# Queries and first gate features of a sparse-attention layer as rounded halves, gate columns first

## The chip, the cores and the metric

The kernel runs on one core of one Trainium2 chip. The metric is the device time of one execution in microseconds (us), lower is better. A run of a kernel gives one such time; the time given for a kernel is the median of its runs.

## The reference, cut to what matters

The reference is one inference step of a small decoder with one mLSTM layer and one sparse-attention layer (NSA), for a prompt of 512 rows and a sample group of 8 x 4 = 32 rows that share every weight. Everything is float32. The change lies in the first part of the attention layer, for all 544 rows x (1024 features each):

```python
h = rmsnorm(x)                        # here: rows x, as 8 slices of 128 features x 544 rows
up = h @ w_in                         # w_in: 1024 x (1024 queries | 3 x 1024 gate features | 48 branch gates)
q  = up[:, 0:1024]                    # 16 heads of 64
z  = silu(up[:, 1024:4096])           # one set of 1024 per branch: compressed, selected, window
g  = sigmoid(up[:, 4096:4144])        # one weight per branch and head
s  = q . kcmp * scale                 # 31 compressed keys per row
p  = masked_softmax(s)
o_cmp = p @ vcmp                      # compressed branch
y  = sum over branches of g * z * o   # later: the selected and window branches, then y @ w_out
```

## The kernel before, in words

The program is a row of stages. Each stage is one block with a program for each of the engines, and a block's end is a barrier for the engines that it uses. Engines meet through semaphores. Big weights come as 28 chunks of up to 2 MB (`weight_chunks`, L63), loaded by SyncE (SP) into a ring of two slots in turn (`wring`, slot = chunk number modulo 2); `load_chunks` (L88) waits, before it loads chunk c, for the last use of chunk c-2 (`chunk_last`), and an engine that reads a chunk waits in `chunk` (L107). PSUM banks go round: `open_bank` (L115) takes the next of `nring` banks (6 in this part) and waits until its former user has emptied it.

Matrix products are done in two ways. Where both operands are float32, one call of the program becomes two weight loads and two passes, so that the trace has two records for each call. In several other stages the operands are split ahead: ScalarE (ACT) rounds a float32 tile to float32r ("high"), VectorE (DVE) subtracts and keeps the rest ("low"), and three float32r products (high x high, high x low, low x high) are added in PSUM, each with one record. The stage of the mLSTM gate path, `stage_gate` (L1200), does it so: its products are L1238 to L1240, its roundings L1259 (weights, 1024 columns) and L1263 (rows, 544 columns), its rests L1280 and L1284.

The stages that the change touches:

- `stage_compress` (L1817) makes the compressed keys and values. At its end SP has already issued the loads of chunks 17 and 18, whose slots are free early.
- `stage_query` (L2053): 8 query pieces of 128 features (chunks 17 and 18, four each), each as two groups of rows (256 and 288), each group 8 float32 calls (L2066); then the 48 branch-gate columns (chunk 19) for five row tiles by `project_rows` (L2072, products at L1317). ACT empties each query bank (L2115, L2120, scaled) and applies the sigmoid to the gates (L2126). DVE only clears `QS`; POOL builds masks. SP loads chunks 19, 20 and 21, each once its slot is free.
- `stage_cmp_branch` (L2238): scores against compressed keys (L2263, L2270), gate features of branch 0, first half (`z_features`, L2142, four pieces, chunk 20), transposes of the weights P (L2278), second half of the gate features (chunk 21), the samples' sums (L2287), and then for each of 8 head pairs t a product that spreads the softmax sums' reciprocals over features (L2297, bank `cR`) and the product P x V (L2303, bank `cP`). DVE makes masked scores, maxima and differences (L2337 to L2348), then sums and reciprocals (L2353 to L2357), copies the transposed P (L2362), and for each t multiplies `cR` by z (L2371) and the result by `cP` (L2374). ACT does the exponentials (L2320) and silu (L2175, L2177). SP loads chunks 22 and 23, then stores the samples' rows in 8 transfers (L2313).
- `stage_keys` (L2377) does the selected and window branches in 64 steps, and the gate features of branches 1 and 2 (chunks 22 to 25) by `z_features` at its start and `z_blocks` between steps. In a gate-feature bank of the kernel before, one call makes 64 features, two of them side by side in the array.

The order of work on an engine is the order of the program text. A chunk's load is one DMA of 128 x 8 rows of 2 KB, by the call

```python
sp.dma_start(dst, src).then_inc(k.chunk_here[c % NW], 16)
```

## Time and profile before

| what | value |
|---|---|
| median of 3 runs | 1504.17 us (1503.64 to 1505.37) |
| the profiled execution's own time | 1504.39 us |
| its span in the trace | 1502.6 us |
| TensorE busy | 1396.2 us, 93% |
| VectorE, ScalarE, GpSimd busy | 50%, 34%, 13% |
| mean granted TensorE clock | 0.96 |
| stage_query | about 943 to 1015 us of the span |
| stage_cmp_branch | about 1015 to 1109 us |

Times are microseconds from the span's start unless marked ns. PE is TensorE's matmul, PEld its weight loads, which overlap PE. "PEq", "SPq" are the engines' sequencers. The mean of one matmul record holds its whole pipeline; records overlap, so what a matmul costs is read from the starts of successive ones or from a group's busy time over its calls. "Idle before, releaser" is the time an engine waited and what ended it; "<-PEq L2871" is the release at a block's end.

### The profile page before, as it was taken

The page shows a single profiled execution, that of the slowest core. Times are in us where ns is not written, and L with a number is a line of the kernel's source. Part 1 is how long each engine was busy: PE and PEld are TensorE (multiplying, and loading weights), DVE is VectorE, ACT ScalarE, POOL GpSimd, SP SyncE. Part 2 cuts the span into 40 slices and gives each one's busy share as a digit, 9 for nine tenths or more (in the row PEclk, how much of TensorE's full clock was granted, in tenths as well). Part 3 has the DMA queues.
Part 4 walks back from the last instruction along what each step waited for, and adds up shares of the span by engine and source line. Part 5 has one row for each costly group of instructions (what it writes and reads, how often), then busy time and mean ns, then how long its engine had stood idle before and what let it go on. Part 6 is the DMA issues. An engine that isn't in the chain of part 4 may idle for free. (4 is left out here: it accounts for less than half of the span.)

```text
span 1502.6 us, 24705 instructions
## 1 busy us (share of the span) xinstructions
PE 1396.2 (93%) x9357; PEld 1002.6 (67%) x9357; DVE 743.9 (50%) x1575; ACT 515.8 (34%) x1227; POOL 189.6 (13%) x231
## 2 busy tenths in 40 slices
PE   4899899999996699999799999999999999999978
PEld 4899655454542599777577999787666555555456
DVE  4676446676755732625633231005034656565646
ACT  5232524242421332423522231122104545454542
POOL 5221041313130100000110110100000000010020
PEclk9999999999998799999899999997999999999999
DMA  6431236767677522222443340011141314141221
GB/s 188 167 113 56 72 105 225 252 221 256 222 257 261 212 84 86 85 102 87 146 170 120 102 165 11 3 60 58 57 124 33 122 52 141 60 113 63 43 93 60
DMA packets 93835, 182.06 MB, mean 121 GB/s; under 512 B 10855, under 2 KB 24835, under 8 KB 92515
## 3 DMA queue, kind: packets, MB, share of 16 engines
q1 hardware_dynamic: 90998, 164.88, 33.4%
q0 software_dynamic: 2720, 15.60, 3.1%
q8 instruction: 76, 1.25, 0.3%
q14 instruction: 41, 0.34, 0.1%
HBM read 133.82 MB, written 54.95 MB: 126 GB/s over the span
## 5 line engine op out<-in xcount | busy, mean ns | idle before, releaser
L1022 DVE SCALAR_TENSOR_TENSOR wring<-wring,nbw,ps 128x512 f32<-128x512 f32 x128 | 86.9, 742 | 59.8 <-PE ps L673 59.7
L2160 PE MATMUL ps<-xnT,wring 128*64 128x256 f32 (+1 forms) x768 | 101.3, 400 | 1.9 <-DVEq L2662 1.7
L2615 ACT ACTIVATE P<-ps,nmx 128x128 f32<-128x128 f32 (+3 forms) x128 | 66.3, 522 | 95.4 <-DVE nmx L2648 95.4
L2142 PE MATMUL ps<-xnT,wring 128*64 128x256 f32 (+1 forms) x768 | 90.4, 398 | 1.3 <-PEq L2874 1.3
L1417 PE MATMUL ps<-wh,xl 128*128 128x512 f32 x224 | 88.1, 393 | 0.0
L416 PE MATMUL ps<-xuh,wuh 128*128 128x256 f32 (+1 forms) x256 | 77.6, 303 | 11.3 <-DVE wring_low L363 10.3
L1238 PE MATMUL ps<-xh,wh 128*128 128x256 f32 (+1 forms) x256 | 75.0, 293 | 7.2 <-DVE xl L1284 7.1
L2142 PEld LDWEIGHTS ps<-xnT,wring 128*64 128x64 f32 x768 | 59.0, 139 | 32.2 <-issue 3.8
L2648 DVE TENSOR_REDUCE nmx<-ps 128x1 f32<-128x128 f32 (+3 forms) x128 | 56.8, 486 | 47.0 <-PE ps L2479 40.8
L417 PE MATMUL ps<-xul,wuh 128*128 128x256 f32 (+1 forms) x256 | 76.3, 298 | 0.0
L418 PE MATMUL ps<-xuh,wring_low 128*128 128x256 f32 (+1 forms) x256 | 76.3, 298 | 0.0
L1239 PE MATMUL ps<-xl,wh 128*128 128x256 f32 (+1 forms) x256 | 74.3, 290 | 0.0
L1240 PE MATMUL ps<-xh,wl 128*128 128x256 f32 (+1 forms) x256 | 73.9, 289 | 0.0
L2160 PEld LDWEIGHTS ps<-xnT,wring 128*64 128x64 f32 x768 | 50.9, 136 | 31.9 <-issue 8.4
L1902 PE MATMUL ps<-cRh,cwh 128*128 128x384 f32 x192 | 67.5, 352 | 0.0
L1370 DVE TENSOR_TENSOR wring_low<-wring,wh 128x512 fp32r<-128x512 f32 x64 | 41.1, 687 | 53.2 <-PE ps L1381 53.2
L1903 PE MATMUL ps<-cRl,cwh 128*128 128x384 f32 x192 | 65.4, 341 | 0.0
L1904 PE MATMUL ps<-cRh,cwl 128*128 128x384 f32 x192 | 65.4, 340 | 0.0
L2066 PE MATMUL ps<-xnT,wring 128*128 128x256 f32 (+1 forms) x256 | 60.6, 401 | 2.2 <-PEq L3096 2.2
L416 PEld LDWEIGHTS ps<-xuh,wuh 128*128 128x128 f32 x256 | 51.3, 200 | 11.8 <-issue 5.3
L2762 POOL TENSOR_TENSOR arena<-arena,tmp 128x512 f32<-128x512 f32 x16 | 20.3, 1271 | 303.5 <-DVEq L2689 303.5
L2066 PEld LDWEIGHTS ps<-xnT,wring 128*128 128x128 f32 x256 | 49.7, 195 | 12.8 <-issue 2.3
(489 smaller groups left out, 3135.3 us busy)
## 6 DMA issues: line engine op xcount, KB each, us to landing
wring<-in_state_C_dram SPq DMA_DIRECT2D x64, 512.0 KB, 5.2
out_dram<-wring SPq DMA_DIRECT2D x64, 512.0 KB, 5.3
wring<-in_a_w_up_dram SPq DMA_DIRECT2D x8, 2048.0 KB, 8.6
wring<-in_b_w_in_dram SPq DMA_DIRECT2D x8, 2048.0 KB, 9.1
wring<-in_a_w_down_dram SPq DMA_DIRECT2D x4, 2048.0 KB, 8.6
craw<-in_cache_kv_dram SPq DMA_DIRECT2D x64, 128.0 KB
arena<-in_cache_kv_dram SPq DMA_DIRECT2D x32, 256.0 KB, 3.9
arena<-in_cache_win_dram SPq DMA_DIRECT2D x8, 1024.0 KB, 6.0
```

What stands on the lines that cost most here:

```text
L416: pe.matmul(b[:, 0:t1 - t0], w_hi, x_hi, start=kt == 0, stop=False)
L417: pe.matmul(b[:, 0:t1 - t0], w_hi, x_lo, start=False, stop=False)
L418: m = pe.matmul(b[:, 0:t1 - t0], w_lo, x_hi, start=False, stop=kt == KD - 1)
L1022: dve.scalar_tensor_tensor(out=c, in0=c, scalar=nbws[:, h % 2, 2 * S + s:2 * S + s + 1], in1=b[:, :], op0=ALU.mult, op1=ALU.add).then_inc( ...
L1238: pe.matmul(out, w_hi, x_hi, start=kt == 0, stop=False)
L1239: pe.matmul(out, w_hi, x_lo, start=False, stop=False)
L1240: m = pe.matmul(out, w_lo, x_hi, start=False, stop=kt == KD - 1)
L1417: m = pe.matmul(b, x_lo, w_hi, start=False, stop=last and kt == KD - 1)
L1902: pe.matmul(b[:, 0:CROW], w_hi, r_hi, start=j == 0, stop=False)
L2066: m = pe.matmul(b[:, 0:t1 - t0], w[:, kt, 128 * m4:128 * m4 + 128], k.xnT[:, kt, t0:t1], start=kt == 0, stop=kt == KD - 1)
L2142: m = pe.matmul(b[64 * par:64 * par + 64, 0:t1 - t0], w[:, kt, x:x + DH], k.xnT[:, kt, t0:t1], start=kt == 0, stop=kt == KD - 1)
L2160: m = pe.matmul(k.ps[64 * par:64 * par + 64, bank, 0:t1 - t0], w[:, kt, x:x + DH], k.xnT[:, kt, t0:t1], start=kt == 0, stop=kt == KD - 1)
```

## The change

1. The order of chunks 17 to 19: the 48 gate columns come first (17), then the two query chunks (18, 19).
2. The 8 query pieces and the 8 gate-feature pieces of branch 0 are done as high and low halves, three float32r products of 128 features (`InHalves`, pieces p = 0 to 15). ACT rounds the rows (8 x 544 columns) and each weight piece (1024 columns), DVE makes the rests; high weights have two slots, low weights are written over the chunk itself. In `stage_query` pieces 0 and 1 are prepared at the start, piece m+2 after the bank of piece m is emptied; in `stage_cmp_branch` ACT rounds piece t+10 after the silu of piece t, and DVE takes its part between softmax steps.
3. The branch gates are projected ahead of the queries.
4. Chunks 20 to 25 (`GATES`: the gate features of all three branches) come as 16 transfers each: [128 partitions, 4 runs, 64 values], so that the two 64-feature halves of a pair lie next to each other.
5. In the compressed branch DVE multiplies P by reciprocal x gate before the transposes (`cr_ready`); the products and banks `cR` and the multiplication by z of those are gone.

The diff, cut to its core:

```diff
--- before.py
+++ after.py
@@ -70,7 +70,7 @@
             out.append(cols(k.w_down[1024 * half:1024 * half + 1024, :], 512 * n, 512))
     out += [cols(k.w_kv, 512 * c, 512) for c in range(3)]
     out += [k.cmp_w1[s].rearrange("(j p) n -> p j n", p=128) for s in range(2)]
-    out += [cols(k.w_in, 0, 512), cols(k.w_in, 512, 512), cols(k.w_in, 4096, 48)]
+    out += [cols(k.w_in, 4096, 48), cols(k.w_in, 0, 512), cols(k.w_in, 512, 512)]
...
 CH_UP, CH_DOWN, CH_KV, CH_CMP, CH_IN, CH_OUT, CH_END = 0, 8, 12, 15, 17, 26, 28
+GATES = range(CH_IN + 3, CH_OUT)
 def load_chunks(sp, k, lo, hi):
@@ -95,6 +96,13 @@
             bank, n_full = k.chunk_last[c - NW]
             sp.wait_ge(k.half_done if bank == "half" else k.w_low if bank == "low" else k.bank_full[bank], n_full)
+        if c in GATES:
+            for par in range(2):
+                for kt in range(KD):
+                    sp.dma_start(dst[:, kt].rearrange("p (hh a d) -> p a hh d", a=2, d=DH)[:, par],
+                                 src[:, kt, 256 * par:256 * par + 256].rearrange("p (hh d) -> p hh d", d=DH)).then_inc(k.chunk_here[c % NW], 16)
+            continue
...
@@ -107,7 +115,8 @@
 def chunk(pe, k, c):
     src = k.chunks[c]
-    pe.wait_ge(k.chunk_here[c % NW], 16 * (c // NW + 1) + (48 if c >= CH_OUT else 0))
+    loads = sum(2 * KD if e in GATES else 4 if e >= CH_OUT else 1 for e in range(c % NW, c + 1, NW))
+    pe.wait_ge(k.chunk_here[c % NW], 16 * loads)
...
@@ -2050,24 +2059,77 @@
+class InHalves:
+    def __init__(self, k, xh, xl, wh):
+        self.k, self.xh, self.xl, self.wh = k, xh, xl, wh
+    def cols(self, p, w):
+        return w[:, :, 128 * (p % 4):128 * (p % 4) + 128]
+    def chunk_no(self, p):
+        return CH_IN + 1 + p // 4
+    def high(self, p):
+        return self.wh[:, p % 2]
+    def low(self, p):
+        return self.cols(p, self.k.wring_low[:, self.chunk_no(p) % NW, :].rearrange("p (a b) -> p a b", b=512))
+    def key(self, p, hf):
+        return ("q", p, hf) if p < 8 else ("z", 0, p - 8, hf)
+    def round_x(self, act, kt):
+        act.activation(self.xh[:, kt, :], self.k.xnT[:, kt, :], ACT.Copy).then_inc(self.k.xq_high, 1)
+    def rest_x(self, dve, kt):
+        dve.wait_ge(self.k.xq_high, kt + 1)
+        dve.tensor_tensor(self.xl[:, kt, :], self.k.xnT[:, kt, :], self.xh[:, kt, :], ALU.subtract).then_inc(self.k.xq_low, 1)
+    def round_w(self, act, p):
+        w = self.cols(p, chunk(act, self.k, self.chunk_no(p)))
+        if p >= 2:
+            bank, n = self.k.bank_of[self.key(p - 2, 1)]
+            act.wait_ge(self.k.bank_full[bank], n)
+        act.activation(self.high(p), w, ACT.Copy).then_inc(self.k.wq_high, 1)
+    def rest_w(self, dve, p):
+        w = self.cols(p, chunk(dve, self.k, self.chunk_no(p)))
+        dve.wait_ge(self.k.wq_high, p + 1)
+        dve.tensor_tensor(self.low(p), w, self.high(p), ALU.subtract).then_inc(self.k.wq_low, 1)
+    def piece(self, pe, p):
+        k = self.k
+        pe.wait_ge(k.wq_low, p + 1)
+        low = self.low(p)
+        for hf, (t0, t1) in enumerate(HALF):
+            b, full = open_bank(pe, k, self.key(p, hf))
+            for kt in range(KD):
+                if p == 0 and hf == 0:
+                    pe.wait_ge(k.xq_low, kt + 1)
+                x_hi, x_lo = self.xh[:, kt, t0:t1], self.xl[:, kt, t0:t1]
+                out = b[:, 0:t1 - t0]
+                pe.matmul(out, self.wh[:, p % 2, kt, :], x_hi, start=kt == 0, stop=False)
+                pe.matmul(out, self.wh[:, p % 2, kt, :], x_lo, start=False, stop=False)
+                m = pe.matmul(out, low[:, kt], x_hi, start=False, stop=kt == KD - 1)
+            m.then_inc(full, 1)
+        k.chunk_last[self.chunk_no(p)] = k.bank_of[self.key(p, 1)]
 def stage_query(nc, k, ctx):
     block = ctx.enter_context(nc.Block())
     SCALE = float(DH) ** -0.5
+    hq = k.hq
     @block.tensor
     def _(pe):
-        for c in range(2):
-            w = chunk(pe, k, CH_IN + c)
-            for m4 in range(4):
-                for hf, (t0, t1) in enumerate(HALF):
-                    b, full = open_bank(pe, k, ("q", 4 * c + m4, hf))
-                    for kt in range(KD):
-                        m = pe.matmul(b[:, 0:t1 - t0], w[:, kt, 128 * m4:128 * m4 + 128], k.xnT[:, kt, t0:t1],
-                                      start=kt == 0, stop=kt == KD - 1)
-                    m.then_inc(full, 1)
-            k.chunk_last[CH_IN + c] = k.bank_of[("q", 4 * c + 3, 1)]
-        project_rows(pe, k, "bg", k.xnT, CH_IN + 2, 1)
+        project_rows(pe, k, "bg", k.xnT, CH_IN, 1)
+        for p in range(8):
+            hq.piece(pe, p)
...
+        hq.round_x(act, 0)
+        hq.round_w(act, 0)
+        for kt in range(1, KD):
+            hq.round_x(act, kt)
+        hq.round_w(act, 1)
+        for i in TILES:
+            r = 128 if i < NT else S
+            b, free = full_bank(act, k, ("bg", i))
+            act.activation(k.gt[0:r, i, :], b[0:r, 0:3 * H], ACT.Sigmoid).then_inc(free, 1)
         act.wait_ge(k.q_clear, 1)
         for m in range(8):
             g = m // 2
@@ -2120,14 +2191,18 @@
                             x = act.activation(k.QS[d0:d0 + 64, odd:SB:2, g, 16 * odd + hh:16 * odd + 16:HPG], rows[:, odd:SB:2, :],
                                                ACT.Copy, scale=SCALE)
                 x.then_inc(free, 1)
-        for i in range(NT + 1):
-            r = 128 if i < NT else S
-            b, free = full_bank(act, k, ("bg", i))
-            act.activation(k.gt[0:r, i, :], b[0:r, 0:3 * H], ACT.Sigmoid).then_inc(free, 1)
+            hq.round_w(act, m + 2)
     @block.vector
     def _(dve):
+        hq.rest_x(dve, 0)
+        hq.rest_w(dve, 0)
+        for kt in range(1, KD):
+            hq.rest_x(dve, kt)
+        hq.rest_w(dve, 1)
         dve.memset(k.QS[:, :, :, :], 0.0).then_inc(k.q_clear, 1)
+        for m in range(8):
+            hq.rest_w(dve, m + 2)
 def z_bank(pe, k, br, c, n):
@@ -2138,7 +2213,7 @@
     b, full = open_bank(pe, k, ("z", br, HPG * c + hh, hf))
     for kt in range(KD):
         for par in range(2):
-            x = 256 * par + DH * hh
+            x = 128 * hh + DH * par
             m = pe.matmul(b[64 * par:64 * par + 64, 0:t1 - t0], w[:, kt, x:x + DH], k.xnT[:, kt, t0:t1],
                           start=kt == 0, stop=kt == KD - 1)
     m.then_inc(full, 1)
...
@@ -2243,9 +2313,9 @@
     Sc = sb("Sc", [128, NT + 1, H, 32])
     Pc = sb("Pc", [128, NT + 1, H, 32])
     PcT = k.kvT.rearrange("p a t -> p (a t)")[:, 0:(NT + 1) * 4 * 128].rearrange("p (i g t) -> p i g t", i=NT + 1, g=4)
-    mx = sb("cmx", [128, NT + 1, H])
-    sm = sb("csm", [128, NT + 1, H])
-    zr = sb("czr", [128, 2, T])
+    x0 = (NT + 1) * D + (NT + 1) * 4 * 128
+    mx, sm = (k.arena[:, x0 + n * (NT + 1) * H:x0 + (n + 1) * (NT + 1) * H].rearrange("p (i h) -> p i h", h=H) for n in range(2))
+    hq = k.hq
     block = ctx.enter_context(nc.Block())
     def heads_of(t):
@@ -2270,14 +2340,16 @@
                 m = pe.matmul(b[32 * g:32 * g + 32, 32 * s:32 * s + NCMP], k.QS[:, s, g, :], k.kcT[:, s, g // 2, :],
                               start=True, stop=True)
         m.then_inc(full, 1)
-        z_features(pe, k, 0, 0)
+        for p in range(8, 12):
+            hq.piece(pe, p)
         for i in range(NT + 1):
-            pe.wait_ge(k.cp_ready, i + 1)
+            pe.wait_ge(k.cp_ready if i == NT else k.cr_ready, i + 1)
             b, full = open_bank(pe, k, ("cT", i))
             for g in range(G if i < NT else 2):
                 m = pe.transpose(b[:, 128 * g:128 * g + 128], Pc[:, i, 4 * g:4 * g + 4, :].rearrange("p h n -> p (h n)"), k.ident[:, :])
             m.then_inc(full, 1)
-        z_features(pe, k, 0, 1)
+        for p in range(12, 16):
+            hq.piece(pe, p)
         drained(pe, k, ("cT", NT))
         for r in range(4):
@@ -2287,16 +2359,9 @@
                     m = pe.matmul(b[32 * g:32 * g + 32, DH * a:DH * a + DH], PcT[32 * r:32 * r + NCMP, NT, a, 32 * g:32 * g + 32],
                                   k.vcS[32 * r:32 * r + NCMP, a, DH * g:DH * g + DH], start=True, stop=True)
             m.then_inc(full, 1)
-        pe.wait_ge(k.cr_ready, 1)
         for i in range(NT):
             drained(pe, k, ("cT", i))
         for t in range(KD):
-            b, full = open_bank(pe, k, ("cR", t))
-            for i in range(NT):
-                for par, h in enumerate(heads_of(t)):
-                    m = pe.matmul(b[64 * par:64 * par + 64, 128 * i:128 * i + 128], sm[:, i, h:h + 1].to_broadcast([128, DH]),
-                                  k.ident[:, :], start=True, stop=True)
-            m.then_inc(full, 1)
             b, full = open_bank(pe, k, ("cP", t))
             for par, h in enumerate(heads_of(t)):
                 g, hh = h // HPG, h % HPG
@@ -2318,8 +2383,11 @@
             act.wait_ge(k.cs_ready, i + 1)
             n = H if i < NT else SB
             act.activation(Pc[:, i, 0:n, :], Sc[:, i, 0:n, :], ACT.Exp).then_inc(k.cp_ready, 1)
-        z_silu(act, k, 0, 0)
-        z_silu(act, k, 0, 1)
+        for t in range(KD):
+            for hf in range(2):
+                z_silu_bank(act, k, 0, t // HPG, t % HPG + HPG * hf)
+            if t < 6:
+                hq.round_w(act, t + 10)
     @block.vector
     def _(dve):
@@ -2355,11 +2423,17 @@
             st.then(dve.reciprocal(m_, m_))
             if i < NT:
                 st.then(dve.tensor_tensor(m_, m_, k.gt[:, i, 0:H], ALU.mult))
-        dve.sem_inc(k.cr_ready, 1)
+                dve.tensor_tensor(Pc[:, i, :, :], Pc[:, i, :, :], m_.unsqueeze(2).to_broadcast([128, H, 32]),
+                                  ALU.mult).then_inc(k.cr_ready, 1)
+            if i in (1, 3):
+                hq.rest_w(dve, 10 + i // 2)
+        hq.rest_w(dve, 12)
         for i in range(NT + 1):
             n = G if i < NT else 2
             b, free = full_bank(dve, k, ("cT", i))
             dve.tensor_copy(PcT[:, i, 0:n, :], b[:, 0:128 * n].rearrange("p (g t) -> p g t", g=n)).then_inc(free, 1)
+        for p in range(13, 16):
+            hq.rest_w(dve, p)
         for r in range(4):
             b, free = full_bank(dve, k, ("cO", r))
             dve.tensor_tensor(k.osb[:, r:SB:4, :], b[:, 0:2 * DH].rearrange("p (a d) -> p a d", d=DH),
@@ -2367,11 +2441,8 @@
         for t in range(KD):
             for hf in range(2):
                 drained(dve, k, ("z", 0, t, hf))
-            b, free = full_bank(dve, k, ("cR", t))
-            st.then(dve.tensor_tensor(zr[:, t % 2, :], b[:, :], k.z[:, t, :], ALU.mult))
-            dve.sem_inc(free, 1)
             b, free = full_bank(dve, k, ("cP", t))
-            dve.tensor_tensor(k.y[:, t, 0:T], b[:, :], zr[:, t % 2, :], ALU.mult).then_inc(free, 1)
+            dve.tensor_tensor(k.y[:, t, 0:T], b[:, :], k.z[:, t, :], ALU.mult).then_inc(free, 1)
 def stage_keys(nc, k, ctx):
@@ -2868,11 +2939,16 @@
         k.identb = sb("identb", [128, 128], BF16, where=att)
         k.causb = sb("causb", [128, 128], BF16, where=att)
         k.newb = sb("newb", [128, NQ * S + 4], BF16, where=att)
-        with ExitStack() as c:
-            k.mtmp = sb("mtmp", [128, 132 + NQ * S], where=c)
-            stage_query(nc, k, c)
-        with ExitStack() as c:
-            stage_cmp_branch(nc, k, c)
+        with ExitStack() as rows:
+            k.hq = InHalves(k, rows.enter_context(nc.sbuf_tensor("xh5", [128, KD, TA], F32R)),
+                            over(nc, "xl5", [128, KD, TA], k.at["arena"]),
+                            rows.enter_context(nc.sbuf_tensor("wh5", [128, 2, KD, 128], F32R)))
+            with ExitStack() as c:
+                k.mtmp = sb("mtmp", [128, 132 + NQ * S], where=c)
+                stage_query(nc, k, c)
+            with ExitStack() as c:
+                stage_cmp_branch(nc, k, c)
         with ExitStack() as c:
             stage_keys(nc, k, c)
     with ExitStack() as c:
```

## Rows read from the trace of the kernel before

**Rows 1.** The page: busy time, share of the span and instructions of each engine

```profile
PE 1396.2 (93%) x9357; PEld 1002.6 (67%) x9357; DVE 743.9 (50%) x1575; ACT 515.8 (34%) x1227; POOL 189.6 (13%) x231
```

**Rows 2.** PE in order of time: start, length, line, operands, count of records

```profile
1004.37 10.25 PE L1317 MATMUL ps<-wring,xnT 128*32 128x48 f32 x80
1015.61 13.86 PE L2263 MATMUL ps<-cmp_rows,Qp 64*128 64x31 f32 x128 [0.99 <-PEq L2871]
...
1030.42 3.89 PE L2142 MATMUL ps<-xnT,wring 128*64 128x256 f32 x18
...
1109.52 29.55 PE L2142 MATMUL ps<-xnT,wring 128*64 128x256 f32 x256 [1.28 <-PEq L2874]
```

**Rows 3.** PE groups by line, window 943 to 1016, then 1015 to 1110

```profile
L2066 PE MATMUL ps<-xnT,wring 128*128 128x256 f32 (+1 forms) x256 | 60.6, 401 | 2.2 <-PEq L3096 2.2
...
L2297 PE MATMUL ps<-ident,csm 128*64 128x128 f32 x128 | 8.6, 273 | 0.0
L2303 PE MATMUL ps<-arena,cmp_rows 128*64 128x512 f32 x32 | 8.5, 592 | 0.0
```

**Rows 4.** PE in order of time in stage_gate: float32r products, first of each group

```profile
550.24 0.30 PE L1238 MATMUL ps<-xh,wh 128*128 128x288 f32 x1
...
553.44 0.28 PE L1238 MATMUL ps<-xh,wh 128*128 128x256 f32 x1
...
556.27 0.30 PE L1238 MATMUL ps<-xh,wh 128*128 128x288 f32 x1
```

**Rows 5.** ACT in order of time: roundings, then the end of a query piece

```profile
505.99 4.47 ACT L1263 ACTIVATE xh<-xnT 128x544 fp32r<-128x544 f32 x8
...
520.59 1.05 ACT L1259 ACTIVATE wh<-wring 128x1024 fp32r<-128x1024 f32 x1
...
1004.47 0.38 ACT L2115 ACTIVATE Qp<-ps 64x256 f32<-64x256 f32 x1 [3.12 <-PE ps L2066]
...
1005.30 0.25 ACT L2120 ACTIVATE QS<-ps 64x16 f32<-64x16 f32 x2
```

**Rows 6.** DVE in order of time: rests in stage_gate, the last score difference

```profile
507.26 6.73 DVE L1284 TENSOR_TENSOR xl<-xnT,xh 128x544 fp32r<-128x544 f32 x5
...
527.70 1.23 DVE L1280 TENSOR_TENSOR wl<-wring,wh 128x1024 fp32r<-128x1024 f32 x1 [0.52 <-ACT wh L1259]
...
1033.74 0.43 DVE L2348 TENSOR_TENSOR Sc<-Sc,cmx 128x256 f32<-128x256 f32 x1
```

**Rows 7.** Windows: us, PE, PEld, DVE, ACT, POOL busy, PEclk, DMA share, GB/s

```profile
944.50:946.00 1.50, 1.50 (x7) 1.28 (x6) 0.35 (x1) 0.00 (x0) 1.07 (x4) 0.74 0.00 0
...
1006.50:1008.00 1.50, 1.50 (x16) 1.50 (x15) 0.00 (x0) 0.56 (x2) 0.00 (x0) 1.00 1.01 345
...
1012.50:1014.00 1.50, 1.50 (x9) 1.50 (x9) 0.00 (x0) 0.00 (x0) 0.00 (x0) 0.50 0.00 0
...
1033.50:1035.00 1.50, 1.50 (x14) 0.94 (x12) 1.37 (x4) 0.78 (x2) 0.00 (x0) 0.85 0.00 0
```

**Rows 8.** SP in order of time, then one source's durations (min/median/max ns)

```profile
1014.65 0.37 SPq L104 DMA_DIRECT2D wring<-in_b_w_in_dram  x1
...
1094.70 4.26 SPq L2313 DMA_DIRECT2D sample_rows<-osb  x8
...
1317.06 3.13 SPq L101 DMA_DIRECT2D wring<-in_b_w_out_dram  x4
...
L101 SPq DMA_DIRECT2D wring<-in_b_w_out_dram x4: 618/665/1056, 1317.1 to 1319.6; - x4
```

**Rows 9.** The mLSTM stage's end: POOL in order of time, ACT's wait (us, times, longest)

```profile
497.93 0.54 POOL L903 DMA_DIRECT2D out_dram<-nprow  x1
...
ACT wh L1259 <- PEq L3069: 4.9, 1, 4.9
```

**Rows 10.** DMA issues: KB each, median us from issue to landing

```profile
wring<-in_b_w_in_dram SPq DMA_DIRECT2D x1, 192.0 KB, 2.8
...
out_dram<-nprow POOLq DMA_DIRECT2D x1, 8.0 KB, 5.1
```

More of the change, by code:

```diff
@@ L2158, in z_blocks @@
         for par in range(2):
-            x = 256 * par + DH * hh
+            x = 128 * hh + DH * par
             m = pe.matmul(k.ps[64 * par:64 * par + 64, bank, 0:t1 - t0], w[:, kt, x:x + DH], k.xnT[:, kt, t0:t1],
@@ L2178, in z_silu_bank @@
     m.then_inc(free, 1)
-def z_silu(act, k, br, c):
-    for n in range(2 * HPG):
-        z_silu_bank(act, k, br, c, n)
 def z_ready(eng, k, br, c):
@@ L3012, in build @@
         k.xr_low = sem("xr_low")
+        k.xq_high = sem("xq_high")
+        k.xq_low = sem("xq_low")
+        k.wq_high = sem("wq_high")
+        k.wq_low = sem("wq_low")
         k.w_high = sem("w_high")
```

## The prediction

> **What bounds the kernel now.** The page first: TensorE (PE) is busy for 93% of the span, no other engine for more than half [rows 1], so time is won where PE's calls get shorter or fewer and lost where PE stands still. Then the two stages that the change touches, by line and in order of time. `stage_query` is 60.6 us of query products [rows 3] and 10.25 us of gate columns [rows 2]; `stage_cmp_branch` is 14.8 us of scores (1015.61 to 1030.42, [rows 2]), eight pieces of gate features, 2 us of transposes and a tail. Between the stages' borders PE has next to no gap, so its order and its durations give the time, as long as nobody feeds it late. Last the windows of 1.5 us: in and behind the gate columns the granted clock is 0.50, half of 2.4 GHz [rows 7], so each moved part has to be priced at the clock that it will find.
>
> **1. The products as halves.** Four float32 pieces at full clock take 29.55 us [rows 2], 7.39 each (the query pieces 60.6 / 8 = 7.58, with a cold start in it [rows 3]). The float32r price is in `stage_gate`, which makes the same shapes: 24 products of 288 columns, from 550.24 to 553.44, take 3.20 us, 24 of 256 from there to 556.27 take 2.83 [rows 4]. A piece becomes 6.03 us with all three products: 1.36 less for each of 16, **21.7 us**.
>
> Can the others keep up? ACT empties a piece's second group in 1.1 us (from 1004.47, [rows 5]) and rounds the next weights in 1.05 [rows 5], DVE takes 1.23 for the rest [rows 6]: 3.4 us from the end of piece m to piece m+2's weights, and PE works 6.03 us on m+1. Hidden, with 2.6 to spare. At the stage's start ACT needs 4.5 + 2 x 1.05 = 6.6 us. DVE took 6.73 / 5 = 1.35 a slice for rests while POOL worked beside it [rows 6]; all eight at that and two weights are 13.3 us, the upper end; without POOL a slice should be 544/1024 of 1.23, 0.65, the lower end 7.7. POOL's masks fill only the first 6 us: I take 10 to 11. The cover is the gate columns, now first; without it 10 us would show. In the branch, piece 10 waits for ACT behind the last exponential and for DVE behind two softmax tiles, some 7 us after the last score difference at 1034.2 [rows 6], at 1041; PE reaches it at about 1044. Piece 11 is due at 1047 and wanted at 1050. The four multiplications of P lie in the same cover. Nothing, and 3 us of slack.
>
> **2. Gate columns first.** Before, they ran at full clock with 16 records per 1.5 us, at half with 9 and then 8.7 on average [rows 7]. Behind the sparse end of `stage_compress` the clock fell at about 945 already [rows 7] and came back only since dense products followed. Now none follow until the 80 records are through: 16 at full clock, 64 at half, 1.5 + 11.0 = 12.5 us for 10.25, **+2.2**. Then piece 0 runs about 3.5 us cold, as the gate features did from 1030.4 to 1034 [rows 2, 7]: +1.75, against 1.5 that the queries lost before, **+0.2**. Pieces 0 to 7 end at 943.85 + 12.5 + 48.2 + 1.75 = 1006.3; before, PE's work in the stage ended at 1014.6 [rows 2].
>
> **3. The 16 transfers of a chunk.** This term decides. Chunks 20 to 25 come as 16 DMAs each instead of one. Landing is no trouble: 1024 pieces of 192 bytes landed in 2.8 us, fixed part included [rows 10], so 8192 of 256 bytes take at most 8 times that, 22 us, and likelier 10 to 15; each of these chunks is wanted 18 us or more after its issue, chunk 20 by PE only 30 us after. The Trainium skill ("DMA: Bandwidth & Descriptors", the table at its head) has a rule against this change, that runs below 512 bytes are read, modified and written; the sum would not move by it, while no run here shows such runs at line rate.
>
> What is not hidden is SP's own time. A chunk's single issue takes 0.37 us [rows 8]. The 4 of a w_out chunk, with a split destination, took 3.13, 0.78 each, the 8 stores of 256-byte rows 4.26, 0.53 each [rows 8]. The new form has 128 partitions of short runs like the stores and a split destination like w_out, whose median is 0.665: I take **0.55 us each, 8.8 us a chunk**; ends 0.37 and 0.78. By the Trainium skill (the same page, the DGE table's 512 cycles per DMA of earlier generations, at 1.2 GHz) it would be an estimated 0.43 us and 6.8 us a chunk, and the result 4 us lower.
>
> Who stands behind it? Chunk 21 may only start when piece 7 is done, chunk 23 when piece 15 is, both at the end of a stage. Before, that place cost one issue: 1014.65 + 0.37 = 1015.02, and PE started at 1015.61 [rows 2, 8]. A block's end waits for every engine: at the mLSTM stage's end ACT stood 4.9 us for POOL's last store [rows 9], issued at 497.93 and landed 5.1 us later [rows 10].
> - First border: SP is through at 1006.3 + 8.8 = 1015.1, ACT and DVE at +3.4. PE starts 0.6 later, 1015.7, where it started before. All of the 8.3 us won in `stage_query` is waited away, and 9 us of standstill lets the clock fall, so the scores take 14.8 as before.
> - Second border: SP's 8.8 and the stores' 4.3 us [rows 8] follow each other, 13.1 plus 0.6. Before, the stores ended at 1098.96, 10 us ahead of the next stage. PE's own tail is 1 us of sample sums and at most 8.5 of cP, the **8.6 of cR** being gone [rows 3]; it and the 16 DVE products of the tail, now 8, would end at 9 to 10 us.
>
> **4. The branch in sequence.** From 1015.7: scores 14.8, pieces 8 to 11 24.1 + 1.75 cold, transposes 2.1, pieces 12 to 15 24.1: 1082.6. Border 13.7: 1096.3, where the next stage started at 1109.5 [rows 2]: 13.2 earlier. PE stands 4 to 5 us before it, the clock falls, and some 4 us of products run at half: 2 us given back. Elsewhere (chunks 22, 24, 25) the 16 issues lie in waits of over 20 us between SP's loads: nothing, and up to 5 us if a load of sample rows came late by them.
>
> **The sum.** 21.7 - 2.2 - 0.2 + 8.6 is 28 us of PE work; at the borders some 15 of it are waited away and 2 go into the clock: **11 us** are left. The profiled execution took 1504.4, so 1493.2; the median lies 0.2 lower: **1493**. A difference of 0.2%, 3 us, is about what a measurement of this kernel tells from none.
>
> **Rivals.**
> - *The borders don't bind (0.2).* For it: 0.37 us is the commonest issue and no row has the new form; against: both rows with split or short runs are over 0.5. At 0.37 each border is 2.9 us shorter: 1487. If SP does not hold the block at all: first border 3.4 + 0.6, 5.3 us won; pieces 8 to 15, 10.7; tail 10 for the 16.3 between 1093.2 and 1109.5, 6.3: together 22, **1482**. With some full clock left for the scores, 1478.
> - *SP's queue is full (0.1, the other side).* The engines' work on 512 pieces holds up each issue. The place is the same two borders, 32 issues; with 11 us to lose it decides from 0.55 + 11/32 = 0.90 us per issue. For it: one w_out issue took 1.06 us [rows 8]. At that price each border is 8.1 us longer: 1493 + 16 = **1509**. Against: 1024 pieces in 2.8 us are 1.4 for 512 with the fixed part, well under 1 without.
> - *Halves starve (0.08).* DVE or ACT come late for pieces 0, 10 or 11, by 2 to 4 us each beyond the slack above. It gives 1497 to 1501.
>
> The rest, 0.62, is the forecast; its own range is 0.45 to 0.75 us per issue, 1490 to 1500. For 8 in 10 the cheap border is added below and the starved halves above: **1482 to 1501**. Faster by over 3 us: 0.62, 0.2 less a little, and half of the third, less some of its upper edge: 0.82; same 0.08; slower 0.10.
>
> **What would show it.** Right: float32r products 118 and 133 ns apart; gate columns 12 to 13 us with the clock at 0.50; ACT and DVE done 3 to 4 us after piece 7, PE idle some 9 us, and SP's 16 issues ending 0.6 us ahead of the scores; at the second border 16 issues and then the 8 stores as the last thing. Wrong: 16 issues in under 6 or over 12 us; a stage starting before SP is through; PE waiting for low weights between pieces; a high clock in the scores.

## The result, and the profile after

| what | before | after |
|---|---|---|
| median of 4 runs | 1504.47 us (1503.64 to 1505.37) | 1495.27 us (1494.29 to 1495.76) |
| ratio, with its 95% interval | | 0.9936 [0.9923, 0.9949] |
| the profiled execution's own time | 1504.39 us | 1495.41 us |
| its span | 1502.6 us | 1493.7 us |
| mean granted TensorE clock | 0.96 | 0.953 |

The changed kernel is 9.2 us faster; the forecast was 1493.0, with 1482 to 1501 around it. The page, first part, to be held against [rows 1]:

```profile
PE 1374.5 (92%) x9229; PEld 1011.5 (68%) x9229; DVE 765.4 (51%) x1595; ACT 535.2 (36%) x1251; POOL 193.0 (13%) x231
```

PE is busy for 21.7 us less, and only 8.9 of them show in the span; the mean clock has fallen too. (That this is the 21.7 of the prediction's step 1 is chance: the removed `cR` products are in it, and products that a lower clock made longer.) Where the rest went is seen in PE's rows in order of time (start, length, line, operands, records, idle before them and its releaser), the same places as [rows 2]:

```profile
945.26 14.31 PE L1326 MATMUL ps<-wring,xnT 128*32 128x48 f32 x80 [2.42 <-PEq L3176]
...
1018.52 3.84 PE L2333 MATMUL ps<-cmp_rows,Qp 64*128 64x31 f32 x34 [9.24 <-PEq L2947]
...
1084.12 0.97 PE L2359 MATMUL ps<-cmp_rows,arena 31*32 31x64 f32 x64
1085.03 7.09 PE L2368 MATMUL ps<-arena,cmp_rows 128*64 128x512 f32 x32
1098.29 1.98 PE L2217 MATMUL ps<-xnT,wring 128*64 128x256 f32 x8 [6.17 <-PEq L2950]
```

Two standstills, 9.24 us ahead of the scores and 6.17 ahead of `stage_keys`, stand where the kernel before had 0.99 and 1.28. Both end with "PEq", the release at a block's end. Who was last in the block is seen in the durations of the new line's issues (min/median/max in ns, first to last), window 1008 to 1020 and window 1083 to 1099, and in SP in order of time behind the second:

```profile
L103 SPq DMA_DIRECT2D wring<-in_b_w_in_dram x16: 367/507/508, 1009.3 to 1017.4; - x16
...
L103 SPq DMA_DIRECT2D wring<-in_b_w_in_dram x16: 368/507/1249, 1084.2 to 1093.3; - x16
...
DMA to landing us min/median/max: 2.3/3.0/3.3
```

```profile
1094.00 3.69 SPq L2378 DMA_DIRECT2D sample_rows<-osb  x8
1098.82 2.67 SPq L2267 DMA_DIRECT2D osall<-sample_rows  x8
```

An issue takes SP 0.507 us (the median; the first took 0.37). The sixteenth of chunk 21 ends at 1017.9, and the scores start 0.6 later. At the second border the 16 issues are followed by the 8 stores to 1097.69, and the next stage starts 0.6 after those. The granted clock around both (windows: us, PE, PEld, DVE, ACT, POOL busy, PEclk, DMA share, GB/s):

```profile
1013.50:1015.00 1.50, 0.00 (x0) 0.00 (x0) 0.00 (x0) 0.00 (x0) 0.00 (x0) 0.50 1.09 239
...
1094.00:1095.50 1.50, 0.00 (x0) 0.00 (x0) 0.00 (x0) 0.00 (x0) 0.00 (x0) 1.00 1.21 234
1098.50:1100.00 1.50, 1.50 (x8) 0.88 (x8) 0.07 (x1) 0.00 (x0) 0.00 (x0) 0.50 0.03 10
```

In the first of these windows nothing works but SP and the transfers, and the clock has fallen to 1.2 GHz; in the second it is still high. Behind the second standstill the products of `stage_keys` also start at 1.2 GHz.

### The profile page after: what moved, and what is told of

The parts are those of the page before. It is cut to its first block and busy times, and to the rows that moved or that the text cites. A ratio compares the mean times of both kernels' runs of the same rounds, so it can differ in the third digit from the quotient of the medians.

```text
span 1493.7 us, 24597 instructions
## 1 busy us (share of the span) xinstructions
PE 1374.5 (92%) x9229; PEld 1011.5 (68%) x9229; DVE 765.4 (51%) x1595; ACT 535.2 (36%) x1251; POOL 193.0 (13%) x231
## 5 line engine op out<-in xcount | busy, mean ns | idle before, releaser
L2235 PE MATMUL ps<-xnT,wring 128*64 128x256 f32 (+1 forms) x768 | 101.3, 400 | 1.5 <-DVEq L2733 1.3
L425 PE MATMUL ps<-xuh,wuh 128*128 128x256 f32 (+1 forms) x256 | 78.9, 308 | 11.3 <-DVE wring_low L372 10.7
L1247 PE MATMUL ps<-xh,wh 128*128 128x256 f32 (+1 forms) x256 | 75.0, 293 | 7.1 <-DVE xl L1293 7.0
L2115 PE MATMUL ps<-xh,wh 128*128 128x256 f32 (+1 forms) x256 | 74.9, 293 | 0.0
L2116 PE MATMUL ps<-xl,wh 128*128 128x256 f32 (+1 forms) x256 | 74.9, 293 | 0.0
L2117 PE MATMUL ps<-xh,wring_low 128*128 128x256 f32 (+1 forms) x256 | 74.6, 291 | 0.0
L1248 PE MATMUL ps<-xl,wh 128*128 128x256 f32 (+1 forms) x256 | 74.3, 290 | 0.0
L2235 PEld LDWEIGHTS ps<-xnT,wring 128*64 128x64 f32 x768 | 50.8, 136 | 31.6 <-issue 8.0
L425 PEld LDWEIGHTS ps<-xuh,wuh 128*128 128x128 f32 x256 | 52.6, 206 | 11.8 <-issue 5.8
L1695 DVE TENSOR_TENSOR cRl<-ps,cRh 128x512 fp32r<-128x512 f32 x36 | 23.2, 686 | 69.3 <-ACT cRh L1688 69.3
```

The costliest lines, as they stand in the source:

```text
L425: pe.matmul(b[:, 0:t1 - t0], w_hi, x_hi, start=kt == 0, stop=False)
L1247: pe.matmul(out, w_hi, x_hi, start=kt == 0, stop=False)
L1248: pe.matmul(out, w_hi, x_lo, start=False, stop=False)
L2115: pe.matmul(out, self.wh[:, p % 2, kt, :], x_hi, start=kt == 0, stop=False)
L2116: pe.matmul(out, self.wh[:, p % 2, kt, :], x_lo, start=False, stop=False)
L2117: m = pe.matmul(out, low[:, kt], x_hi, start=False, stop=kt == KD - 1)
```

## The experiments

Theory A is what step 3 of the prediction says: SP's issue time, not the transfers' landing, holds both borders. Later ones ask what the other parts are worth once the borders are free. All ratios are to the kernel before, whose median was 1505.3 to 1506.0 us beside these runs (7 to 13 runs) and 1504.5 beside the first ones. Differences between two experiments are given from their medians; by the ratios they come out up to 1 us otherwise.

**e1: the two loads away from the borders.** Chunk 21 is loaded by the branch's stage and chunk 23 by `stage_keys`, each as its first load, still with 16 transfers.

```diff
-        load_chunks(sp, k, CH_IN + NW, CH_IN + 3 + NW)
+        load_chunks(sp, k, CH_IN + NW, CH_IN + 2 + NW)
...
-        load_chunks(sp, k, CH_IN + 3 + NW, CH_IN + 5 + NW)
+        load_chunks(sp, k, CH_IN + 2 + NW, CH_IN + 4 + NW)
...
+        load_chunks(sp, k, CH_IN + 4 + NW, CH_IN + 5 + NW)
         fetch_samples(sp, k, 0)
```

> Chunks 21 and 23 (still 16 transfers each) are issued at the start of the next stage instead of at the end of theirs. Theory A (SP's issue time holds the two borders): the scores start about 5 us earlier, ACT's and DVE's last preparation of piece 9 being what is left (3.4 us after piece 7, plus 0.6), and the next stage after the compressed branch about 4.5 us earlier (DVE's last product plus 0.6); together 9 to 12 us less than the changed kernel, 1484 to 1486. Rival B (the borders last as long as they do for another reason: engines draining, or PE restarting cold): no change, 1495. Rival C (the loads come too late for piece 12 or for the first gate blocks): a new PE wait in the middle of a stage, 1495 or more.

Measured: 1484.34 us (1481.21 to 1487.31), ratio 0.9864 [0.9847, 0.9882]. PE at the two borders, in order of time:

```profile
1008.48 12.82 PE L2333 MATMUL ps<-cmp_rows,Qp 64*128 64x31 f32 x128 [3.99 <-PEq L2948]
...
1083.52 1.73 PE L2217 MATMUL ps<-xnT,wring 128*64 128x256 f32 x14 [1.31 <-PEq L2951]
```

The standstills are 3.99 and 1.31 us where they were 9.24 and 6.17. The 3.99 left at the first is ACT and DVE on piece 9's weights behind the last query bank, 3.4 + 0.6 by step 1 of the prediction. DVE is through with them at 1008.0, half a us ahead of the scores:

```profile
1006.78 1.23 DVE L2102 TENSOR_TENSOR wring_low<-wring,wh 128x1024 fp32r<-128x1024 f32 x1 [4.74 <-ACT wh L2097]
```

**e2: 32 transfers of 64 KB a chunk**, each of the 16 cut in two.

```diff
+                    for h2 in range(2):
-                    sp.dma_start(dst[:, kt].rearrange("p (hh a d) -> p a hh d", a=2, d=DH)[:, par],
-                                 src[:, kt, 256 * par:256 * par + 256].rearrange("p (hh d) -> p hh d", d=DH)).then_inc(k.chunk_here[c % NW], 16)
+                        sp.dma_start(dst[:, kt].rearrange("p (hh a d) -> p a hh d", a=2, d=DH)[:, par, 2 * h2:2 * h2 + 2],
+                                     src[:, kt, 256 * par + 128 * h2:256 * par + 128 * h2 + 128].rearrange("p (hh d) -> p hh d", d=DH)).then_inc(k.chunk_here[c % NW], 16)
```

> Each chunk of gate features comes as 32 transfers of 64 KB instead of 16 of 128 KB; the pieces of 256 bytes and their number stay. Theory A (time of SP's issues, 0.51 us each): 16 more issues at each border, 8.2 us each, 16 to 17 us more than the changed kernel, 1511 to 1512. Rival C (what holds the border is the transfer of the 8192 pieces, not the issue): 0 to 1 us more, 1495 to 1496. Rival B (neither): 1495.

Measured: 1509.86 us (1506.71 to 1513.64, 10 runs), ratio 1.0033 [1.0021, 1.0044]: slower than the kernel before, and a little under the 1511 expected, since the smaller issues are shorter. PE in order of time, then SP's durations at the first border:

```profile
1023.72 4.65 PE L2334 MATMUL ps<-cmp_rows,Qp 64*128 64x31 f32 x41 [17.09 <-PEq L2948]
...
1111.99 2.40 PE L2218 MATMUL ps<-xnT,wring 128*64 128x256 f32 x10 [13.70 <-PEq L2951]
```

```profile
L104 SPq DMA_DIRECT2D wring<-in_b_w_in_dram x32: 367/469/477, 1006.7 to 1022.7; - x32
```

The same bytes in the same runs of 256 bytes; only the count of issues has doubled, and each standstill grew by 7.5 to 8 us. Half the size saves SP 38 ns an issue, so it is mainly the issue that costs, not its bytes. SP is through at 1023.2 and the scores start at 1023.7.

**e3: one transfer a chunk.** Chunks 20 to 25 are loaded as before the change, and ACT and DVE read the weights of a piece as two runs of 64 columns instead. The rests, which can no longer lie over the piece's own columns, go into memory that is free there.

```diff
-        if c in GATES:
+        if False:
...
+    def raw(self, p, w):
+        return w.rearrange("p k (a hh d) -> p hh k a d", a=2, d=DH)[:, p % 4] if p >= 8 else self.cols(p, w)
...
+        if p >= 8:
+            return self.wl[2 if p == 15 else p % 2][:, :, :]
...
-            x = 128 * hh + DH * par
+            x = 256 * par + DH * hh
```

> Gate-feature chunks come in one transfer of 2 KB rows, as in the kernel before; ACT and DVE read a piece's weights as two runs of 64 and write them side by side, the rests into free memory. Theory A: the two SP terms shrink to 0.37 us each; first border 3.9 us (ACT, DVE), second about 9.5 us after piece 15; the next stage starts almost warm; 10 to 12 us less than the changed kernel, 1483 to 1485. Rival B: 1495. Rival D (reading in runs of 64 makes ACT and DVE slower, so that pieces wait): float32r pieces over 6.2 us each, 1488 or more.

Measured: 1484.28 us (1482.57 to 1485.95), ratio 0.9861 [0.9845, 0.9878]. PE in order of time:

```profile
946.60 9.67 PE L1326 MATMUL ps<-wring,xnT 128*32 128x48 f32 x80 [2.42 <-PEq L3186]
...
1009.74 12.84 PE L2342 MATMUL ps<-cmp_rows,Qp 64*128 64x31 f32 x128 [3.99 <-PEq L2957]
...
1085.03 2.34 PE L2225 MATMUL ps<-xnT,wring 128*64 128x256 f32 x19 [1.31 <-PEq L2960]
```

The same standstills as e1 to 0.01 us and the same time, by another road: behind the border the 16 issues of e1 cost nothing. And the new layout of the chunks is not needed at all, and its 16 issues cost the change about 11 us (1495.27 - 1484.28; 14 by the second median of the changed kernel, e10). Here the 80 records of the gate columns took 9.67 us for the 14.31 of the changed kernel, with not a line of them edited; more on that below.

**e4: the `cR` products put back** into the changed kernel: 128 products by PE and 8 multiplications by DVE in the tail, the four multiplications of P gone.

```diff
-                dve.tensor_tensor(Pc[:, i, :, :], Pc[:, i, :, :], m_.unsqueeze(2).to_broadcast([128, H, 32]),
-                                  ALU.mult).then_inc(k.cr_ready, 1)
...
         for t in range(KD):
+            b, full = open_bank(pe, k, ("cR", t))
+            for i in range(NT):
+                for par, h in enumerate(heads_of(t)):
+                    m = pe.matmul(b[64 * par:64 * par + 64, 128 * i:128 * i + 128], sm[:, i, h:h + 1].to_broadcast([128, DH]),
+                                  k.ident[:, :], start=True, stop=True)
+            m.then_inc(full, 1)
```

> The changed kernel with the products of the softmax sums (cR) and DVE's multiplication of them by z put back; P isn't scaled ahead. Theory A: PE's tail grows by 7 us (8.6 busy, overlapping), but SP's 8.5 + 3.7 us stand beside it: the border after the branch moves only by what exceeds them, 15.0 + 1.2 against 14.0, so about 2 us more than the changed kernel, minus up to 2 for a warm start of the next stage: 1495 to 1498. Rival (SP doesn't bound this border): the whole 7 to 8 us, 1502 to 1503.

Measured: 1494.65 us (1493.42 to 1496.91), ratio 0.9924 [0.9907, 0.994], which can't be told from the changed kernel. Its tail, by PE and SP in order of time:

```profile
1082.58 0.97 PE L2361 MATMUL ps<-cmp_rows,arena 31*32 31x64 f32 x64
1098.91 2.38 PE L2217 MATMUL ps<-xnT,wring 128*64 128x256 f32 x20 [1.31 <-PEq L2961]
```

```profile
1082.68 10.87 SPq L103 DMA_DIRECT2D wring<-in_b_w_in_dram  x16
1093.72 3.69 SPq L2387 DMA_DIRECT2D sample_rows<-osb  x8
```

PE's tail and SP's tail run beside each other. From the sample sums to the next stage it is 16.3 us here and 14.2 in the changed kernel, but with PE at work to the end the clock stays up, and the first 256 products take 29.5 us for 32.0: 45.8 against 46.2. The removal of `cR` is worth nothing that these runs can tell while SP holds the border.

**e5: the same in e3**, where SP holds nothing.

```diff
+            for i in range(NT):
+                for par, h in enumerate(heads_of(t)):
+                    m = pe.matmul(b[64 * par:64 * par + 64, 128 * i:128 * i + 128], sm[:, i, h:h + 1].to_broadcast([128, DH]),
```

> The products cR put back into the kernel with plain loads, where SP no longer holds the border. Theory A (cR is worth what it costs wherever SP isn't behind it): PE's tail grows from about 8 to 15 us, so 6 to 7 us more than the kernel with plain loads (1484.3): 1490 to 1491. Rival (removing cR is worth nothing, because scaling P ahead costs DVE as much): 1484 to 1485.

Measured: 1489.04 us (1487.62 to 1492.33), ratio 0.989 [0.9868, 0.9912]. The tail takes 16.3 us (1078.4 to 1094.7) where e3's takes 9.3, both with 29.5 behind it: 7.0 us. By the medians it is 4.8, with intervals of 2.5 and 3.3 us, so a little less than expected. The same edit is worth nothing or 5 to 7 us, by what stands beside it.

**e6: the query pieces as float32 calls**, in e3; only the gate features keep the halves.

```diff
+        if p < 8:
+            w = self.cols(p, chunk(pe, k, self.chunk_no(p)))
+            for hf, (t0, t1) in enumerate(HALF):
+                b, full = open_bank(pe, k, self.key(p, hf))
+                for kt in range(KD):
+                    m = pe.matmul(b[:, 0:t1 - t0], w[:, kt, :], k.xnT[:, kt, t0:t1], start=kt == 0, stop=kt == KD - 1)
```

> The kernel with plain loads, with the 8 query pieces as float32 calls of 128 columns again and the gate features of branch 0 still as halves. Theory A (the halves' gain is PE time per piece, 7.39 less 6.03): 8 x 1.36 = 10.9 us more than 1484.3, 1495; the cold start costs the same. Rival (with ACT and DVE relieved of six roundings the stage runs more smoothly, and part of the halves' gain had been lost in waits): 1490 or less.

Measured: 1493.79 us (1490.81 to 1494.18), ratio 0.9921 [0.9904, 0.9937], 9.5 us over e3. From piece 0's first product to the scores it took 64.4 us for 53.7, 10.7 more; step 1 gives 8 x 1.36 = 10.9. Its products, by line:

```profile
L2123 PE MATMUL ps<-xnT,wring 128*128 128x256 f32 (+1 forms) x256 | 60.4, 400 | 0.0
```

60.4 us, near the 60.6 of [rows 3].

**e7: the gate columns behind piece 0**, in e3, so that nothing covers the preparation of rows and weights. ACT's sigmoids of the gates move behind piece 0's bank to match.

```diff
-        project_rows(pe, k, "bg", k.xnT, CH_IN, 1)
-        for p in range(8):
+        hq.piece(pe, 0)
+        project_rows(pe, k, "bg", k.xnT, CH_IN, 1)
+        for p in range(1, 8):
             hq.piece(pe, p)
```

> The kernel with plain loads, with the gate columns after query piece 0 instead of ahead of all. Theory A (gate columns first cost little, since they cover the preparation of the rows): PE waits for the rests of the rows in piece 0, which then takes 11 to 13 us, the gate columns take about 10 (a warm first half), and piece 1 starts cold: 2 to 3.5 us more than 1484.3, 1486 to 1488. Rival (the cold clock in the gate columns is the dearer part, and moving them behind dense products wins it back): 3 to 4 us less, 1480 to 1481.

Measured: 1487.87 us (1487.01 to 1490.02), ratio 0.9879 [0.9862, 0.9895], 3.6 us over e3. PE at the stage's start:

```profile
949.68 0.38 PE L2123 MATMUL ps<-xh,wh 128*128 128x256 f32 x1 [5.02 <-DVE wring_low L2110]
...
958.03 4.24 PE L1326 MATMUL ps<-wring,xnT 128*32 128x48 f32 x45
```

PE stands 5.02 us for the first low weights, and piece 0 then takes 8.35 us for 6.03 (the rests of the rows' slices and a low clock both lie in it and weren't taken apart). Columns first looks like the cheaper order: by 3.6 us of the medians (2.7 by the ratios), and in the profiles the stage up to the scores takes 72.1 us for 65.6 in e3. How much is open, for e3's gate columns were among the quick ones (see e10); in e5, whose columns were slow, the same stage takes 70.4.

**e8: piece 9's weights prepared in the next stage**, in e3. The 3.99 us of e3's first border are ACT's and DVE's work for piece 9, which PE wants 20 us later. It goes to the head of the branch's stage.

```diff
-            hq.round_w(act, m + 2)
+            if m < 7:
+                hq.round_w(act, m + 2)
...
-        for m in range(8):
+        for m in range(7):
             hq.rest_w(dve, m + 2)
...
     def _(act):
+        hq.round_w(act, 9)
         for i in range(NT + 1):
...
+        hq.rest_w(dve, 9)
         for i in range(NT + 1):
```

> The kernel with plain loads, with the rounding and the rest of piece 9 moved from the end of the query stage into the compressed branch (ACT at its start, DVE behind the score differences). Theory A (with SP away, ACT and DVE hold the first border with 2.3 us of preparation): the scores start 2.0 to 2.3 us earlier, 1482, less what the clock takes. Rival (DVE's later softmax makes piece 10 or 11 wait): the gain is lost there, 1484 to 1485.

Measured: 1477.14 us (1473.86 to 1479.9), ratio 0.9814 [0.9789, 0.9839], the fastest of all. It is 7.1 us under e3 where 2.3 were expected. PE at the first border, and two windows of the scores:

```profile
1007.54 10.77 PE L2343 MATMUL ps<-cmp_rows,Qp 64*128 64x31 f32 x128 [1.57 <-PEq L2960]
```

```profile
1008.50:1010.00 1.50, 1.50 (x32) 1.50 (x31) 1.50 (x1) 1.28 (x1) 0.00 (x0) 1.00 1.02 382
...
1011.50:1013.00 1.50, 1.50 (x17) 1.50 (x17) 1.29 (x4) 0.00 (x0) 0.00 (x0) 0.50 1.01 378
```

The standstill is 2.4 us shorter, as expected. Behind it the clock was still 1.00 for the scores' first 3 us, 32 records in 1.5 us for 17 at half, and the scores took 11.8 us for 13.9: another 2.1 us. That the shorter standstill is the cause of this isn't shown. Behind the same 3.99 us the clock was high for the scores' first 1 to 2 us in e1 and e3 and low from their start in e5 and e7, and in e9, behind 1.57 us as here, it fell within their first microsecond. Then 1.0 in the branch, less than the 1.4 between two profiles of the changed kernel (50.7 and 52.1 us from the scores' end to the sample sums). Of the last 2.7 us (of 8.1 between the two profiled executions), 1.9 lie in the last stage, which takes 58.7 to 58.8 us in seven of the profiles and 60.5 to 60.9 in five, the changed kernel with one in each group. So 2.4 us are shown to be the edit's; up to 2.1 more may be, and the rest is the kernel's own spread. Its four runs fall into two pairs, 1474 and 1480.

**e9: the scores mixed with gate features**, in e8, to keep the clock up through them: one half of piece 8 each behind score tiles 1 and 2. ACT's and DVE's work on pieces 9 to 11 moves to match, and 8 banks go round instead of 6.

```diff
                         m.then_inc(banks[par][1], 1)
+            if i in (1, 2):
+                hq.piece(pe, 8, (i - 1,))
```

> The kernel with plain loads and late piece 9, with the scores of the compressed branch taken apart: tiles 0 and 1, first half of piece 8, tile 2, second half, tile 3, samples; two more PSUM banks in this stage, and pieces 9 to 11 prepared between the score tiles. Theory A (the scores cost 13.5 us, 10.4 in the last kernel, because the clock falls in them; with dense products between it stays high): from the scores' start to the samples' sums 56 to 58 us instead of 62.9, 5 to 7 us less than 1477, 1470 to 1472. Rival (DVE, with some 32 us of work ahead of the transposes, bounds this stretch): PE waits for low weights or at the transposes, 59 us or more, 1473 to 1477.

Measured: 1478.77 us (1477.49 to 1484.61, 5 runs), ratio 0.9831 [0.9814, 0.9849]: no gain over e8, so the theory fell. A wait of PE (us, times, longest) and a window tell why:

```profile
PE ps L2124 <- ACT z L2261: 4.3, 1, 4.3
```

```profile
1035.00:1038.00 3.00, 1.45 (x6) 1.45 (x7) 2.76 (x9) 2.13 (x5) 0.00 (x0) 0.50 0.00 0
```

ACT's silu of piece 8 now stood behind the exponentials, the bank came free late, PE stood 4.3 us in the middle of the branch and the clock fell there. ACT in its turn had waited for DVE's score differences, 2.1 to 6.2 us before each exponential, so the rival has the better of it, though PE waited for a bank and not for low weights. Nor did the edit hold the clock up in the scores, where it had fallen before the first half piece came:

```profile
1011.00:1014.00 3.00, 3.00 (x31) 3.00 (x31) 2.19 (x4) 1.03 (x1) 0.00 (x0) 0.50 1.04 406
```

From the scores' start to the sample sums it took 70.1 us for 62.9 in e8. This profile is of one of the two longer of the five runs, 1484.07 us.

**e10: the changed kernel once more**, with no edit, for its spread.

> The changed kernel unchanged, beside the others. It tells how much of a few us between kernels is the clock's luck in the gate columns: in the traces so far these took 9.7 us in five kernels and 12.8 to 14.3 in three, with nothing changed in them. Theory A (where the fall of the clock comes is set by what ran before and by chance): times spread over 3 to 5 us, median 1493 to 1496. Rival (the changed kernel always meets the slow case): a spread under 2 us.

Measured: 1498.12 us (1496.4 to 1500.54, 5 runs), ratio 0.9953 [0.9939, 0.9966], with the kernel before at 1505.31 there. Its gate columns took 13.00 us:

```profile
946.48 13.00 PE L1326 MATMUL ps<-wring,xnT 128*32 128x48 f32 x80 [2.42 <-PEq L3176]
```

The runs spread over 4.1 us, as theory A has it, but their median lies 2 us above its range. The two medians of the changed kernel are 2.9 us apart with nothing changed. So the gain is 7 to 9 us, and differences under 3 us between experiments are not leaned on here.

## Why the prediction was right

**The products as halves (step 1): right.** The halves save 10.7 us on eight pieces in e6 (10.9 worked out), with the float32 pieces at 60.4 us as before. The other eight were not undone by themselves; the branch from the scores' end to the sample sums took 50.7 us, for 52.05 in step 4's working (and 52.1 in e10). Of the cover, only DVE's rate was mis-stated. In the changed kernel, DVE, then POOL, in order of time:

```profile
947.73 4.72 DVE L2090 TENSOR_TENSOR xl<-xnT,xh 128x544 fp32r<-128x544 f32 x7
```

```profile
946.59 1.39 POOL L2149 TENSOR_SCALAR_AFFINE_SELECT mtmp<-mtmp 32x128 f32<-32x128 f32 x1
```

A slice's rest took 4.72 / 7 = 0.67 us, the lower of my two ends (0.65 and 1.35), though POOL worked beside it; it was POOL that was held up. The 1.35 of [rows 6] was a mean of two rates, and beside other work of POOL's (below). No piece waited for low weights. The rival in which the halves starve is out: e7 shows what it looks like.

**The gate columns (step 2): right in kind, 1.8 us too small.** 12.5 us were worked out with 16 of the 80 records at full clock. They took 14.31: at 947.5 the clock was at half already, and it came back only in piece 0, near 963:

```profile
947.50:949.00 1.50, 1.50 (x9) 1.50 (x8) 1.50 (x3) 1.50 (x4) 1.21 (x3) 0.50 0.00 0
...
962.50:964.00 1.50, 1.50 (x10) 1.50 (x10) 0.00 (x0) 0.00 (x0) 0.00 (x0) 0.66 1.05 408
```

But this is no fixed price: the same code took 9.6 to 9.8 us in five of the traces and 13.0 to 14.4 in five others. In the first five the granted clock fell 6.2 to 6.3 us after the columns' first record, in the others 1.1 to 2.6 us after it. I took the clock of one profiled execution for a property of the place. The size of the term was within its spread, yet a spread of 5 us was not in my working, and is larger than the term itself.

**The transfers (step 3): right, and it decided.** 0.507 us an issue for 0.55; 8.6 us for 16 at the first border for 8.8; standstill 9.24 for 9; the scores 0.6 us behind SP's last issue, as worked out. The start came at 1018.5 for 1015.7: 1.4 from a later start of the stage, 1.8 from the gate columns, less 0.4 in pieces and issues. e1 and e3 remove the standstill in two ways, e2 doubles it. The rival "the borders don't bind" is out, and its 1482 is what e1 and e3 came near to (1484). The full queue, which needed 0.90 us an issue, is out at this form: none at the first border was over 0.51, and at the second one of sixteen took 1.25 (up to 2.0 in e4 and e10), which leaves a mean of 0.60 to 0.68. One row that step 3 leans on fits its rule less well: POOL's store had landed at 503.0, and ACT was let go at 505.0, not 0.6 us behind it, so that this store held that border isn't shown. For the two borders here e1 to e3 show it.

**The second border and `cR`: right in sum, and more so than I had seen.** 14.2 us for 13.7, with the stores last; 3.7 us of stores for 4.3, 9.6 of issues for 8.8. I had written the removal of `cR` as 8.6 us of gain and then 15 us as waited away. e4 shows that the two cancel wholly: the removal gave back what it saved, as a standstill and a cold start. The term itself was too large: 8.6 us is the busy time of records that overlap, and where PE is last the removal is worth 7.0 (e5).

**The next stage (step 4): right.** It started at 1098.3 for 1096.3, the 2.8 late at the first border less 1.3 in the branch plus 0.5 at the second. The cold start cost 32.0 - 29.5 = 2.5 us for 2. The 2.0 of the later start and these 0.5 are the distance between the forecast and the profiled execution, 1493.2 and 1495.41, but for 0.3 the other way in stages that the change doesn't touch. That the forecast came so near is in part luck: the gate columns alone move a profile by up to 4.7 us, and the branch, 1.3 us short here, took its 52.1 in e10. The second median, 1498.12, is 5 us above the forecast, still in its range.

So of the 28 us of PE work that the prediction adds up, 9 arrived and 11 went into SP's 32 issues at two borders (e1, e3). 2.4 more went into piece 9's preparation (e8), with up to 2.1 of clock behind it, and 1.6 were never there (`cR`). The 2 to 4 left are of the size of the gate columns' spread and were not taken apart.

## What to carry to other kernels

A transfer cut into pieces to save an engine a stride is paid on the issuing engine's sequencer, here 0.5 us a piece, and it shows in full where that queue holds the end of a stage; ask for each load that waits for a stage's last use whether the next stage could issue it. Before work is removed from the end of a stage, look at who else works there: the same removal was worth nothing with SP last and 5 to 7 us with PE last. A long standstill is dearer than its length, since the clock falls in it: at the second border the 256 products behind 6 to 14 us of it took 1.3 to 2.8 us more (changed kernel, e10, e2) than behind 1.3 us, in all nine other profiles. And a stage's time in one profile is a sample: ask for a second profile of the same kernel before a few us in it are called the edit's.

## What the runs showed of the hardware

- An issue of 128 partitions x 4 runs of 64 values took SP 0.507 us, one of half as many runs 0.469, and one of 128 x 8 rows of 2 KB 0.37 [rows 8], but 0.59 to 0.60 for chunks 24 and 25, which `stage_keys` loads with the same call. The Trainium skill ("DMA: Bandwidth & Descriptors", the table at its head) says that runs under 512 bytes are read, modified and written. In the changed kernel they came with 234 and 239 GB/s in the two windows shown of the standstills, each piece landed within 3.3 us, and chunk 21 was all there 11.2 us after its first issue; e3's single transfer of the same chunk landed in 7.7 us, at up to 410 GB/s. That doesn't price the rule: 128 KB each 0.507 us are 258 GB/s, so SP's issues set the pace there.
- DVE's subtraction of two operands and POOL get in each other's way, and which of them pays depends on POOL's work. The same operation of POOL in the kernel before, DVE idle, was quick:

```profile
945.29 0.30 POOL L2087 TENSOR_SCALAR_AFFINE_SELECT mtmp<-mtmp 32x128 f32<-32x128 f32 x1
```

  0.30 us before, 1.39 after, and all of the masks 10.4 us for 6.2, while DVE's slices beside it took 0.71 to 0.82 us each. It was hidden, so it cost nothing. In [rows 6] POOL did not make masks but subtracted slices of the same rows itself. DVE's five, then POOL:

```profile
L1284 DVE TENSOR_TENSOR xl<-xnT,xh x5: 711/1868/1880, 507.3 to 513.3; 128x544 fp32r<-128x544 f32 x5
```

```profile
507.26 5.51 POOL L1254 TENSOR_TENSOR xl<-xnT,xh 128x544 fp32r<-128x544 f32 x3 [8.79 <-ACT xh L1263]
```

  Three of DVE's slices took 1.87 us and two, the first and the last, 0.71 to 0.72: the 1.35 that I took as the rate beside POOL is their mean.
- The clock in a stretch of thin products is not the same from one execution to the next: 80 records took 9.6 us or 14.4, without an edit to them. A difference of 3 us between two single profiles is within that.
